# First modulation blocks of two streams: products and sums on VectorE beside the input phases, GpSimd's units placed later

## What is computed

```
s_lat = silu(c);  s_ctx = silu(c_ctx)
for layer in range(2):
    shift, scale, gate       = split(s_lat @ w_mod[layer] + b_mod[layer], 3)
    shift_c, scale_c, gate_c = split(s_ctx @ w_mod[layer] + b_mod[layer], 3)
    x_in = x * (1 + scale) + shift;   c_in = h_ctx * (1 + scale_c) + shift_c
    p = x_in @ w_in;  pc = c_in @ w_in         # input phases of layer 0
    ...                                        # convolution, attention, gates, @ w_out
    x = post_norm(x, gate * y);  h_ctx = post_norm(h_ctx, gate_c * y_ctx)
# second block, layers 2 and 3: the same with w_ada_2[l] and one stream
```

## Time and profile before

| | us |
|---|---|
| median of 3 runs | 2838.55 |
| lowest, highest | 2832.22, 2839.12 |
| the profiled execution | 2837.41 |
| its span, first to last instruction | 2835.6 |
| PE busy | 2697.0 |
| DVE busy | 1648.7 |
| GpSimd busy | 1663.2 |
| ACT busy | 1197.5 |

### The profile page before, as it was taken

How to read it: one execution, slowest core, us unless ns; L and a number is a source line. 1 busy time by engine, 2 the same in 40 slices (tenths; PEclk the granted TensorE clock), 3 DMA queues, 4 the chain that set the end, 5 groups by cost and what they waited for, 6 DMA issues and landing times.

```text
span 2835.6 us, 49284 instructions
## 1 busy us (share of the span) xinstructions
PE 2697.0 (95%) x21319; PEld 2458.9 (87%) x21319; DVE 1648.7 (58%) x1907; ACT 1197.5 (42%) x1406; POOL 1663.2 (59%) x875
## 2 busy tenths in 40 slices
PE   5799999999999999999999969999999899999999
PEld 3489988888889999978999958999889889998799
DVE  2344444553444657686676655764776557646763
ACT  0233444333333334334567354633454355434452
POOL 0057777997778799888556803064578450456520
PEclk8699999999999999999999979999999999999999
DMA  9999998998888997767555835665567756655565
GB/s 338 283 314 265 266 265 253 276 289 243 242 241 231 279 276 229 210 203 212 161 150 159 233 100 178 166 177 142 168 182 216 195 158 167 175 142 164 169 183 154
DMA packets 842265, 599.09 MB, mean 211 GB/s; under 512 B 22071, under 2 KB 764865, under 8 KB 841537
## 3 DMA queue, kind: packets, MB, share of 16 engines
q1 hardware_dynamic: 838224, 582.83, 71.1%
q10 hardware_dynamic: 3824, 13.11, 1.2%
HBM read 589.46 MB, written 6.29 MB: 210 GB/s over the span
## 4 chain that ended last, share of the span: by engine, by line
PE 77%; DVE 8%; DMA 6%; POOL 5%; ACT 2%; SPq 1%; issue 1%; DVEq 0%; POOLq 0%; ACTq 0%
PE G L2393 53%; PE G L2412 4%; DMA ring<-in_w_mod_dram 3%; POOL ring L828 3%; PE A L2350 2%; DVE ring_r L1470 2%; POOL mod_rows L836 1%; DMA const<-in_w_mod_dram 1%; PE A L2477 1%; PE A L2483 1%; POOL ring L835 1%; PE A L2480 1%; PE A L2661 1%; PE G L2499 1%; PE G L2642 1%
## 5 line engine op out<-in xcount | busy, mean ns | idle before, releaser
L828 POOL TENSOR_SCALAR ring<-ring,act_in 128x512 f32<-128x512 f32 x448 | 961.7, 2158 | 1024.7 <-DMA ring<-in_w_ada_dram 798.3
L2393 PE MATMUL G<-H_r,ring_r 128*128 128x256 f32 x9008 | 1496.5, 286 | 35.0 <-DVE S_r L1459 19.2
L2393 PEld LDWEIGHTS G<-H_r,ring_r 128*128 128x128 f32 x9008 | 1307.8, 191 | 60.6 <-issue 42.0
L1470 DVE TENSOR_TENSOR ring_r<-ring,ring_r 128x2048 fp32r<-128x2048 f32 x346 | 825.3, 2387 | 280.3 <-ACT ring_r L869 279.2
L869 ACT ACTIVATE ring_r<-ring 128x2048 fp32r<-128x2048 f32 x346 | 661.9, 1913 | 373.7 <-PE G L2393 81.0
L2393 PE MATMUL G<-M_r,ring_r 128*128 128x256 f32 x4464 | 773.0, 284 | 0.0
L2393 PEld LDWEIGHTS G<-M_r,ring_r 128*128 128x128 f32 x4464 | 635.0, 191 | 9.4 <-issue 8.6
L2393 PE MATMUL G<-S_r,ring_r 128*128 128x256 f32 x1536 | 437.5, 285 | 0.0
L836 POOL TENSOR_TENSOR mod_rows<-mod_rows,ring 128x512 f32<-128x512 f32 x196 | 331.4, 1691 | 15.4
L835 POOL TENSOR_TENSOR ring<-ring 128x512 f32<-128x512 f32 x196 | 325.1, 1659 | 16.3
L2393 PEld LDWEIGHTS G<-S_r,ring_r 128*128 128x128 f32 x1536 | 296.1, 193 | 0.1
(11 more groups left out here) (446 smaller groups left out, 2634.7 us busy)
## 6 DMA issues: line engine op xcount, KB each, us to landing
ring<-in_w_in_dram SPq DMA_DIRECT2D x120, 1024.0 KB, 5.5
ring<-in_a_w_in_dram SPq DMA_DIRECT2D x98, 1024.0 KB, 6.9
ring<-in_w_ada_dram SPq DMA_DIRECT2D x192, 512.0 KB, 6.3
const<-in_w_mod_dram SPq DMA_DIRECT2D x192, 256.0 KB, 5.4
ring<-in_c_w_in_dram SPq DMA_DIRECT2D x48, 1024.0 KB, 5.8
ring<-in_w_mod_dram SPq DMA_DIRECT2D x16, 2048.0 KB, 18.0
ring<-in_a_w_out_dram SPq DMA_DIRECT2D x32, 1024.0 KB, 6.2
ring<-in_w_out_dram SPq DMA_DIRECT2D x32, 1024.0 KB, 6.1
```

The lines of the kernel that those rows point to most:

```text
L828: g.mark(pool.tensor_scalar(w[:, i, :], w[:, i, :], act_in[:, k, c:c + 1], None, ALU.mult))
L1470: v.tensor_tensor(w_low(tl), w_raw(tl), w_up(tl).bitcast(F32), ALU.subtract).then_inc(w_lo, 1)
L2393: ins = pe.matmul(G[tl.bank][:, 0:SEQ], w, x, start=(k == 0 and n_ == 0), stop=(k == KT - 1 and n_ == 2))
```

## The change

The 192 units that PE multiplied are now multiplied by DVE. For each unit DVE makes four instructions of 128x256: for both rows x and both streams i it adds `w[:, x, :] * act_in[:, k, i]` to the sum `gemv_sums[:, i, :]` in SBUF (`scalar_tensor_tensor`; `tensor_scalar` for a block's first row). `gemv_part(q, 0)` stands behind `lower` in the loop over tiles and `gemv_part(q, 1)` behind the next attention step: two units in each of the tiles 2 to 97. When a block is complete, PE turns the two sums into four 128x128 pieces in `A[3]` (four transposes for two products before), and DVE sums each piece over its 128 rows with one `tensor_reduce` of 128x512. ACT's copy of each block is gone. The third buffer and the sums take the places of constants that are loaded later. The buffers of the units are now freed by DVE.

GpSimd's units come as 7 for 8 tiles up to tile 97 (78 units by then, 90 before), and as 4 for 5 tiles after it (18 for 25 before). Up to tile 137 they were 118 and are 110, so from tile 98 to 137 they were 28 and are 32. The folding of the norm's gain into the modulation (`fold_norm`) moves from ahead of `ac_out` to its tile 8.

```diff
 def gemv_units_by(q):
-    begin = [10 + 11 * n // 3 for n in range(GEMV_BLOCKS + 1)]
-    return sum(min(8, max(0, -(-8 * (q + 1 - a) // (b - a)))) for a, b in zip(begin, begin[1:]))
+    return min(GEMV_UNITS, max(0, 2 * (q - GEMV_FIRST)))
 def pool_units_by(q):
-    first = max(0, min(q, 97) - 7)
+    first = 7 * max(0, min(q, 97) - 7) // 8
     working = max(0, q - 97) - sum(97 < p <= q for p in PAUSED)
-    return min(POOL_UNITS, first + 18 * working // 25)
+    return min(POOL_UNITS, first + 4 * working // 5)
...
                 if m >= 3:
-                    sp.wait_ge(gemv_used, m - 2)
+                    for i in range(2):
+                        sp.wait_ge(gemv_sum[i], 2 * (m - 2))
...
-                    mod_store(*MOD_BLOCKS[n], three(G[(q - 1) % 2], BW), 2, gemv_out)
+                    V(v.tensor_reduce(cols[:, 40:44], A[3][:, :].rearrange("p (t x) -> p t x", x=P), AX.X, ALU.add))
+                    mod_store(*MOD_BLOCKS[n], cols[:, 40:44].rearrange("p (t i) -> p t i", i=2), 2, gemv_out)
...
+            def gemv_part(q, u):
+                m = 2 * (q - GEMV_FIRST) + u
+                if 0 <= m < GEMV_UNITS:
+                    n, w = m // 8, gemv_unit(m)
+                    v.wait_ge(gemv_full[m % 3], 16 * (m // 3 + 1))
+                    if m % 8 == 0 and n:
+                        v.wait_ge(gemv_cols, n)
+                    for x in range(2):
+                        k = 2 * (m % 8) + x
+                        for i in range(2):
+                            a = act_in[:, k, i:i + 1]
+                            if k == 0:
+                                ins = v.tensor_scalar(gemv_sums[:, i, :], w[:, x, :], a, None, ALU.mult)
+                            else:
+                                v.wait_ge(gemv_sum[i], KT * n + k)
+                                ins = v.scalar_tensor_tensor(out=gemv_sums[:, i, :], in0=w[:, x, :], scalar=a,
+                                                             in1=gemv_sums[:, i, :], op0=ALU.mult, op1=ALU.add)
+                            ins.then_inc(gemv_sum[i], 1)
...
                     chain.upto(2 * j)
                     lower(q0 + j + LEAD)
+                    gemv_part(q0 + j, 0)
                     chain.upto(2 * j + 1)
+                    gemv_part(q0 + j, 1)
...
-                        ins = pe.matmul(A[3][o:o + 32, 0:BW], act_all[:, 3 * k:3 * k + 32], gemv_unit(m)[:, i, :],
-                                        start=(k < 4), stop=(k >= KT - 4), skip_group_check=True)
-                    ins.then_inc(gemv_used, 1)
...
+                    for i in range(2):
+                        pe.wait_ge(gemv_sum[i], KT * (n + 1))
...
+                    for t in range(2):
+                        for i in range(2):
+                            c = 2 * t + i
+                            ins = pe.transpose(A[3][:, c * P:(c + 1) * P], gemv_sums[:, i, t * P:(t + 1) * P], ident)
+                    ins.then_inc(gemv_cols, 1)
```

More of the change, by code:

```diff
@@ L122, in unit_tiles @@
     return tiles
-GEMV_TILE, POOL_TILE = unit_tiles(gemv_units_by, GEMV_UNITS), unit_tiles(pool_units_by, POOL_UNITS)
-GEMV_AT, GEMV_COLS_AT, MOD_COLS_AT = {}, {}, {}
-for _m in range(GEMV_UNITS):
-    GEMV_AT.setdefault(max(GEMV_TILE[_m] - 2, 1), []).append(_m)
-for _n in range(GEMV_BLOCKS):
-    GEMV_COLS_AT[max(GEMV_TILE[8 * _n + 7] - 2, 1) + 1] = _n
+POOL_TILE = unit_tiles(pool_units_by, POOL_UNITS)
+GEMV_COLS_AT = {gemv_tile(8 * _n + 7) + 1: _n for _n in range(GEMV_BLOCKS)}
+MOD_COLS_AT = {}
 for _p in range(len(POOL_BLOCKS)):
@@ L531, in build @@
         late_in = sem("late_in")
-        gemv_used, gemv_rows, gemv_cols, gemv_out = sem("gemv_used"), sem("gemv_rows"), sem("gemv_cols"), sem("gemv_out")
+        gemv_cols, gemv_out = sem("gemv_cols"), sem("gemv_out")
+        gemv_sum = [sem(f"gemv_sum{i}") for i in range(2)]
         pool_used, pool_cols, pool_out = sem("pool_used"), sem("pool_cols"), sem("pool_out")
@@ L905, in _ @@
             upper(1)
-            def gemv_rows_out(n):
-                act.wait_ge(gemv_used, 8 * n + 8)
-                if n:
-                    act.wait_ge(gemv_cols, n)
-                act.activation(gemv_rows_at, A[3][:, 0:BW], ACT.Copy).then_inc(gemv_rows, 1)
             def load_back(i):
@@ L1704, in pairs, with fold_norm @@
                 return mod[:, at:at + 2 * KT].rearrange("p (k i) -> p k i", i=2)
-            V.mark(v.tensor_tensor(pairs(0), pairs(MOD_AT[1] + 2 * KT), both("ln_g"), ALU.mult))
-            V(v.tensor_tensor(pairs(2 * KT), pairs(MOD_AT[1] + 2 * KT), both("ln_b"), ALU.mult))
-            V(v.tensor_tensor(pairs(2 * KT), pairs(2 * KT), pairs(MOD_AT[1]), ALU.add))
-            for name in ("ln_g", "ln_b"):
-                at = ROWS[name][0]
-                V(v.tensor_scalar(pcol[:, at:at + KT], pcol[:, at:at + KT], ALPHA, None, ALU.mult))
+            def fold_norm():
+                v.wait_ge(gemv_out, GEMV_BLOCKS)
+                V.mark(v.tensor_tensor(pairs(0), pairs(MOD_AT[1] + 2 * KT), both("ln_g"), ALU.mult))
+                V(v.tensor_tensor(pairs(2 * KT), pairs(MOD_AT[1] + 2 * KT), both("ln_b"), ALU.mult))
+                V(v.tensor_tensor(pairs(2 * KT), pairs(2 * KT), pairs(MOD_AT[1]), ALU.add))
+                for name in ("ln_g", "ln_b"):
+                    at = ROWS[name][0]
+                    V(v.tensor_scalar(pcol[:, at:at + KT], pcol[:, at:at + KT], ALPHA, None, ALU.mult))
             for phase, x, s, chain in (("ac_out", XH, 1, Pace(turn_y())), ("ax_out", X256, 0, Pace(norm(0, XH, H_hi)))):
@@ L1720, in _ @@
                     mod_event(FIRST[phase][0] + j)
+                    if phase == "ac_out" and j == 8:
+                        fold_norm()
                     chain.upto(2 * j + 1)
@@ L2335, in _ @@
                         ins.then_inc(x_t, 1)
[L2337 to L2352 removed]
             def after_first_half(q):
                 if q in GEMV_COLS_AT:
[L2357 to L2361 removed]
+                    n = GEMV_COLS_AT[q]
+                    for i in range(2):
+                        pe.wait_ge(gemv_sum[i], KT * (n + 1))
+                    if n == 0:
+                        pe.wait_ge(first_used, SHIFT_SCALE)
+                    else:
+                        pe.wait_ge(gemv_out, n)
+                    for t in range(2):
[3 more added lines that the diff above has]
+                    ins.then_inc(gemv_cols, 1)
                 if q - 1 in MOD_COLS_AT:
@@ L2367, in after_first_half @@
                         bank = A[3]
+                        pe.wait_ge(gemv_out, GEMV_BLOCKS)
                         pe.wait_ge(pool_out, p)
```

32 lines of the change are left out of this document (6 added, 26 removed).

## The result

The changed kernel took **3498.9 us** (median of 4 runs, 3478.7 to 3514.3), against 2835.4 for the kernel before, run beside it (2829.4 to 2839.1): a ratio of **1.234 [1.227, 1.241]**. The forecast was 2923 us with a range of 2835 to 3005: the direction was right, the size was not. A loss of 86 us was forecast, and 663 us were lost (660 between the two profiled executions, 3497.4 and 2837.4).

A forecast was written before the change was run, and what follows sets the result against it. TensorE bounds the head stretches now; after the change VectorE's and GpSimd's mutually exclusive SBUF work was to bound the input phases. 2837.4 + 70 (input phases) + 16 (GpSimd's later units) = 2923 us, range 2835 to 3005.

The forecast's parts named there:

- the holds: VectorE and GpSimd exclude each other from SBUF: 3.0 us per GpSimd unit in which VectorE can't work on two SBUF inputs.
- Part 1: Head stretches: TensorE loses its 384 products and alone would need 234 and 257 us, against 251 and 275.
- The rival's -66: Faster case, chance 0.14: TensorE's need decides in the input phases, 66 us less; with 16 us added, 2787.
- +16: Cost in us of four more GpSimd units in tiles 98 to 137, half of 33 us.
- the 34.7 us: TensorE's total wait for the DMAs of its units in the kernel before; the faster case took half, -17.
- Part 2: VectorE's eight new instructions per tile: 0.40 us from start to start, 3.2 us a tile; a block's reduction 0.69 us.
- Part 3: Input phases: VectorE's and GpSimd's work that can't overlap sums to 891 us against 849; at 97% packing 919, +70.
- Part 4: Tiles 98 to 137: GpSimd has 32 units instead of 28, costing 33 us or nothing; half taken, +16.
- Part 5: New waits, of VectorE for a unit's DMA and TensorE for VectorE's last sum, show the +70 and add nothing.
- the +70: Input phases: loss in us from VectorE's and GpSimd's non-overlapping work at 97% packing, 919 against 849.
- GpSimd is starved: Rival: VectorE's 5.5 us runs keep GpSimd out, units come late, SP's queue and weights stand still; 3034 us, chance 0.15.
- Held for the full instruction: Rival: GpSimd's multiplications keep VectorE out for their whole length, 5.7 us a unit; 3137 us, chance 0.02.

The follow-up runs named there:

- number 1: Changed kernel, but SyncE queues each of VectorE's units one tile later: 2953.5 us, ratio 1.042.
- 7: Changed kernel with units queued one tile later and GpSimd's products and sums on 8 columns in place of 512: 2819.5 us, ratio 0.993.
- number 9: Changed kernel in its own order, but only the first three units loaded and multiplied again and again, no wait of SyncE for VectorE: 2906.3 us, ratio 1.024.
- number 10: Changed kernel with only three units loaded, no SyncE wait for VectorE, and 15 of 16 new VectorE products on 8 columns: 2784.3 us, ratio 0.980.
- number 8: Changed kernel with units queued one tile later, a tile's first unit ahead of the lowering, and GpSimd's old spread: 2928.5 us, ratio 1.033.
- number 4: Kernel before with only the new spread of GpSimd's units; the 192 units stay on TensorE: 2831.0 us, ratio 0.998.
- 5: Changed kernel with units queued one tile later and a tile's first unit ahead of the lowering in VectorE's loop: 2927.4 us, ratio 1.032.
- 11: Changed kernel, complete, with VectorE's units issued from ScalarE's queue in place of SyncE's: 2947.7 us, ratio 1.039.

## Why the prediction was wrong, by its own steps

**What bounds, and the holds.** Right in kind. That VectorE and GpSimd keep each other out was read from single instructions, and numbers 1, 7 and 9 show it in the large: 138 ns in the mean on a product, and a mean of 2.39 us for GpSimd's multiplications, of which about 0.4 us are new against the first head stretch of the kernel before. In the changed kernel itself it had all but gone, because the engines were mostly idle. VectorE's products are at their undisturbed length, and GpSimd's multiplications are faster than before (first VectorE's products; then GpSimd's multiplications, in the kernel before from 216 to 467 us and in the changed one from 262 to 736 us):

```profile
L1528 DVE SCALAR_TENSOR_TENSOR const<-const,act_in 128x256 f32<-128x256 f32 x720 | 297.0, 482 | 0.2
```

```profile
L828 POOL TENSOR_SCALAR ring<-ring,act_in 128x512 f32<-128x512 f32 x58 | 112.6, 1953 | 55.3 <-DMA ring<-in_w_mod_dram 48.1 <-DMA ring<-in_w_ada_dram 6.7
...
L832 POOL TENSOR_SCALAR ring<-ring,act_in 128x512 f32<-128x512 f32 x52 | 80.7, 1564 | 335.8 <-DMA ring<-in_w_mod_dram 335.8
```

The forecast had expected these times above their present mean and called itself wrong "if GpSimd's mean times stay as they are"; they fell. It had also said that VectorE would be busy for over 80% in the head stretches; it was for 199 of 474 us in the first (262 to 736 us), 42%.

**Part 1, TensorE's relief.** Supported where nothing covers it. The rival's -66 with +16 for GpSimd gave 2787, and number 10 took 2784. That close a match is luck: the +16 was not there, and number 10 leaves out more than TensorE's products. One term of the -66 was also misread: the 34.7 us of the earlier trace rows are 12.9 of TensorE's products and 21.8 of its weight loads, which waited at the same time: 21.8 in all. The forecast held that none of the relief would show, and no complete version with the products on VectorE was faster than the kernel before.

**Part 2, VectorE's instructions.** The step of 0.40 us was exact. A row of eight, in order of time, in the changed kernel:

```profile
312.83 3.25 DVE L1528 SCALAR_TENSOR_TENSOR const<-const,act_in 128x256 f32<-128x256 f32 x8
```

Seven steps and an instruction of 0.48: (3.25 - 0.48) / 7 = 0.40, although each waits for the sum of the last but one. The reduction of a block's columns took 0.69, as taken.

**Part 3, the sum of the holds.** Its result holds for the kernel that it describes: 919 us forecast for the input phases, 910 measured in number 9, and 2906 in all where the sum gave 2923. But its terms are less sure than this. Its stretches hold 92 tiles and 76 units, where 96 tiles have products and 78 units come; by its own prices some 19 us are missing, and 891 should have been 910, the 919 then 938. And by number 8 a unit more costs 1.1 us and not 3.0, so the holds are not added in full in every place. Errors of both signs are in the sum, and that it fits to 9 us is partly luck.

**Part 4, GpSimd's later units.** +16 was too much: the tiles 98 to 137 took 1 us more in number 4, and in all that kernel was faster. In the changed kernel they took 19 more (282 against 263), and between numbers 8 and 5, which differ in the spread alone, 6 more; why it was 19 was not tried. The sentence of this part that mattered was another: "SP's wait for GpSimd's buffer is passed by the weights of the next tile". It was true of GpSimd's buffer, and I didn't ask the same of VectorE's.

**Part 5, new waits. This is the step that failed.** It named VectorE's wait for a unit's DMA and TensorE's for the sums, and disposed of the third in one sentence: "A unit's buffer is freed a tile ahead of its use." Ahead of its use, yes; but the load that waits for it stands in SyncE's queue ahead of the weights of the next tile, and the products that it waits for stand in VectorE's order behind the lowering of this one. The two waits that it did price were held to be places in which the +70 appears, and SyncE's was put at nothing. It was a cost of its own: 545 us came back with one tile (number 1), 551 with another queue (11), 593 with no such wait at all (9). Two things could have been read ahead of the run. The first is in the diff: a unit queued in the turn of tile q was used in tile q-2 (`GEMV_AT`), and is now used in q-1 (`gemv_tile`), so its buffer comes free a tile later as SyncE counts. Number 1 takes back this one tile. The second is the circle itself: load, products, wait, next load, with everything that stands ahead of each step in its queue, closes on the weights. The forecast looked at how much work each engine has, and summed it; a loop is not seen in sums, since in it nobody has much to do.

**The rivals.** "GpSimd is starved" had the sentence that SP's queue and the weights stand still, but for GpSimd's buffers and at 3034 us. "Held for the full instruction" fell: number 9, where all the work of both engines is done and SyncE never waits for VectorE, took 2906 us, and this rival had 3137.
The single durations say the same: a multiplication that kept VectorE out for all its 1.57 us would make a product of 2.05 us (an estimate, 1.57 + 0.48), and the slowest of number 1's 720 took 1.56.
The Trainium skill's rule ("SBUF — State Buffer", section "Who interferes with whom") is an exclusive lock; its words "for the whole instruction" stand there beside VectorE's 2-port modes, and of an instruction with two SBUF inputs, like these products, it says only that it contends. That they contend is borne out (626 against 488 ns in numbers 1 and 7); for GpSimd's multiplications "the whole instruction" is not.

## What to carry to other kernels

When a buffer's release moves from one engine to another, follow that one buffer around its whole circle: what stands ahead of the release in the new engine's order, and what stands behind the wait in the queue that issues the next load. If the load behind the wait feeds what stands ahead of the release, there is a loop, and its length is the sum of all its parts, however idle the engines are. A load that must wait is queued as late as its use allows, or from a queue behind which nothing urgent stands; here one tile later was worth 545 us.

## What the runs showed of the hardware that was not expected

**TensorE's clock fell while it waited for the loop.** The granted clock was 0.79 in the mean of the input phases, where it was 0.95 to 1.00 before. Windows of 4 us of the changed kernel (columns as in the earlier trace rows):

```profile
304.00:308.00 4.00, 0.00 (x0) 0.00 (x0) 0.00 (x0) 2.27 (x2) 1.26 (x1) 0.68 0.43 115
308.00:312.00 4.00, 0.00 (x0) 0.00 (x0) 2.31 (x5) 3.79 (x7) 0.00 (x0) 0.50 0.00 0
312.00:316.00 4.00, 0.00 (x0) 0.00 (x0) 4.00 (x9) 0.00 (x0) 0.00 (x0) 0.50 0.05 14
316.00:320.00 4.00, 3.81 (x22) 3.85 (x23) 0.94 (x3) 0.00 (x0) 0.29 (x1) 0.62 0.95 285
320.00:324.00 4.00, 1.20 (x11) 1.00 (x9) 0.00 (x0) 0.29 (x1) 3.92 (x3) 1.00 0.80 225
...
332.00:336.00 4.00, 4.00 (x36) 4.00 (x35) 0.16 (x1) 0.14 (x1) 0.00 (x0) 1.00 1.07 295
```

TensorE stood idle while it waited for weights, and the clock fell to 0.50, which is the level of 1.2 GHz; when TensorE had worked again, from 316 us on, it was back at 1.00 (2.4 GHz) in the window of 320 us. TensorE was busy for 2776 us in all, more than in the kernel before, with 768 instructions fewer (2697 us in 21319 before); the 4464 products from `M_r` took 300 ns in the mean and 284 before. How much of the 593 us this is was not taken apart. TensorE's tiles are only 3% of the last chain in the input phases, which speaks for a small share.

**A chain that waits for itself costs nothing extra on VectorE.** Products of 0.48 us that each wait on a semaphore for the last but one began every 0.40 us. They overlap by 0.08 us, as much as neighbours without such a wait do.

**GpSimd slows VectorE's products by much, but seldom and never for long.** The same instruction of 128x256 took 482 ns in the mean with the engines mostly waiting, 626 in number 1, and 488 again there with GpSimd's operations made narrow. The median was 475 to 479 ns in all three, and in no run did a product take over 1.6 us, some 1.1 more than by itself.
